# Expert visits of three token groups: a pair in half rows and a third group in quarter rows

## What is computed

```python
top_val, top_idx = lax.top_k(t @ w_router + b_router, 4)        # 4 of 32 experts for each token
g = jnp.minimum(xb @ w_gate[e] + b_gate[e], 7.0)
u = jnp.clip(xb @ w_up[e] + b_up[e], -7.0, 7.0)
act = g * jax.nn.sigmoid(1.702 * g) * (u + 1.0)
y = act @ w_down[e] + b_down[e]                                 # each of the three is 1024 x 1024
out = out.at[row_tok].add(y * row_w[:, None])
```

## Time and profile before

| | us |
|---|---|
| median of 3 runs | 1359.2 |
| lowest, highest | 1358.0, 1360.04 |
| the profiled execution, its own time | 1355.8 |
| its span (first to last instruction) | 1354.0 |
| TensorE matmul busy | 1295.7 |
| VectorE busy | 485.8 |
| ScalarE busy | 212.3 |
| GpSimd busy | 175.7 |

### The profile page before, as it was taken

The page is one execution under the profiler, slowest core; times in us unless marked ns, Lnnn a source line. Parts: engine busy times, 40 slices in busy tenths (PEclk is TensorE's granted clock), DMA queues, the critical chain, the costliest instruction groups (busy, mean ns, idle before and its releaser), DMA issues.

```text
span 1354.0 us, 25510 instructions
## 1 busy us (share of the span) xinstructions
PE 1295.7 (96%) x10704; PEld 630.4 (47%) x10704; DVE 485.8 (36%) x1124; ACT 212.3 (16%) x458; POOL 175.7 (13%) x138
## 2 busy tenths in 40 slices
PE   8999989998999999999999999999999998999995
PEld 3455565565554555555454543333333333344342
DVE  1875586755322222322322222322331322242221
ACT  2132244331101001110111110110110001001010
POOL 0031320001202120110110220010010010011002
PEclk9999999997899999999999999999999999999998
DMA  9300520236999999999999999999999999999996
GB/s 375 125 1 0 189 79 1 79 139 248 336 353 394 408 404 407 411 404 413 408 409 414 410 409 411 416 405 418 417 406 418 418 403 418 414 413 399 413 412 245
DMA packets 77924, 448.26 MB, mean 331 GB/s; under 512 B 13080, under 2 KB 16392, under 8 KB 28656
## 3 DMA queue, kind: packets, MB, share of 16 engines
q1 hardware_dynamic: 63936, 426.51, 76.8%
q0 software_dynamic: 13296, 17.98, 5.6%
q10 hardware_dynamic: 576, 2.10, 0.4%
HBM read 442.61 MB, written 14.94 MB: 338 GB/s over the span
## 4 chain that ended last, share of the span: by engine, by line
PE 59%; SPq 26%; DVE 6%; DMA 5%; issue 2%; ACT 1%; POOL 1%; POOLq 0%; ACTq 0%; DVEq 0%
PE pair L2027 38%; SPq L701 26%; PE pair L1857 4%; PE pair L1759 4%; PE pair L1720 3%; DMA ring<-in_w_gate 2%; DMA ring<-in_w_down 2%; DVE rest L1168 2%; PE pair L1981 2%; DVE rest L1199 1%; PE pair L1953 1%; PE pair L1994 1%; PE pair L1715 1%; DVE rest L1417 1%; POOL ring L812 1%
## 5 line engine op out<-in xcount | busy, mean ns | idle before, releaser
L2027 PE MATMUL pair<-ring,rest 128*32 128x256 f32 (+1 forms) x7952 | 833.8, 444 | 19.9 <-DMA ring<-in_w_down 12.9
L2027 PEld LDWEIGHTS pair<-ring,rest 128*32 128x32 f32 (+1 forms) x7952 | 332.6, 118 | 437.1 <-issue 288.9
L1168 DVE TENSOR_TENSOR rest<-pair,rest 128x512 f32<-128x512 f32 (+3 forms) x133 | 100.0, 755 | 421.7 <-PE pair L2027 386.6
L870 POOL DMA_INDIRECT out<-rest x57 | 89.7, 1573 | 742.9 <-ACT rest L1125 637.7
L1125 ACT ACTIVATE rest<-rest 128x256 f32<-128x256 f32 (+1 forms) x57 | 31.8, 596 | 512.2 <-DVE rest L1168 512.2
L1107 ACT ACTIVATE rest<-rest 128x512 f32<-128x512 f32 (+3 forms) x34 | 24.4, 718 | 304.6 <-DVE rest L1532 304.6
L1486 DVE TENSOR_SCALAR rest<-pair,rest 96x1 int32<-96x1 f32 (+2 forms) x34 | 7.3, 214 | 178.4 <-PE pair L1953 167.0
L1759 PE MATMUL pair<-ring 128*128 128x512 f32 (+1 forms) x192 | 69.4, 521 | 0.0
L1168 DVE TENSOR_TENSOR rest<-rest 128x512 f32<-128x512 f32 (+8 forms) x85 | 57.1, 683 | 32.1 <-ACT rest L1107 26.7
L2027 PE MATMUL pair<-rest 128*32 128x256 f32 (+1 forms) x592 | 62.1, 439 | 1.8 <-DMA rest<-in_w_down 1.8
L1720 PE MATMUL pair<-ring 128*128 128x512 f32 x128 | 58.1, 613 | 5.8 <-DMA ring<-in_w_in 5.8
(11 more groups left out here) (192 smaller groups left out, 841.3 us busy)
## 6 DMA issues: line engine op xcount, KB each, us to landing
ring<-in_w_gate SPq DMA_DIRECT2D x121, 1024.0 KB, 23.8
ring<-in_w_down SPq DMA_DIRECT2D x121, 1024.0 KB, 27.4
ring<-in_w_up SPq DMA_DIRECT2D x119, 1024.0 KB, 27.7
rest<-in_w_up SPq DMA_DIRECT2D x9, 1024.0 KB
rest<-in_w_gate SPq DMA_DIRECT2D x7, 1024.0 KB
rest<-in_w_down SPq DMA_DIRECT2D x7, 1024.0 KB
ring<-in_w_in SPq DMA_DIRECT2D x8, 520.0 KB, 8.5
ring<-in_x SPq DMA_DIRECT2D x8, 512.0 KB, 13.0
```

The lines of the kernel that those rows point to most:

```text
L870: p.indirect_dma_start(out=out_halves if w == HW else out_rows, out_offset=bass.IndirectOffsetOnAxis(ap=sidx[vi.ring][:, n:n + 1].bitcast( ...
L1168: return v.tensor_tensor(out=out, in0=a, in1=b, op=op)
L2027: last = T.matmul(ps[q * tn:(q + 1) * tn, col:col + w], x, pieces[slot][:, kk, q * w:(q + 1) * w], start=(k == 0 and col % 512 == 0), stop ...
```

## The change

Visits with three groups now have one pair and one single instead of three singles. Where a visit has a single beside its pair, each half of the pair is done by two stationaries of 32 tokens with the same 512 columns, instead of one of 64 tokens. Then a k-step has four matmuls of 32 tokens and 512 columns (partitions from 0, 32, 64 and 96) and four of 32 tokens and 256 columns. Visits with one, two, four groups and the overflow loop are as before. By way of `pairs` the same visits get two result parts instead of three: in `index`, `replicate`, `places`, `plus_bias`, `weigh`, `scatter` and `biases`.

```diff
-        scattered = [sum(g if (g := VISITS[w][1]) % 2 else g // 2 for w in range(v)) for v in range(NV + 1)]
+        scattered = [sum((VISITS[w][1] + 1) // 2 for w in range(v)) for v in range(NV + 1)]
 
         def pairs(vi):
-            return 0 if vi.j is None or vi.G % 2 else vi.G // 2
+            return 0 if vi.j is None else vi.G // 2
...
-                    blocks = {(0, 4): gm_c[:, 2:6], (2, 0): gm_c[:, 0:2], (0, 3): gm_c[:, 2:5],
+                    blocks = {(0, 4): gm_c[:, 2:6], (2, 0): gm_c[:, 0:2], (1, 1): gm_c[:, 0:5:4],
                               (0, 1): gm_c[:, 2:3]}[pairs(vi), singles(vi)]
...
+                            step = TOK if singles(vi) else tn
                             for q in range(DM // w):
-                                last = T.matmul(ps[q * tn:(q + 1) * tn, col:col + w], x,
-                                                pieces[slot][:, kk, q * w:(q + 1) * w],
-                                                start=(k == 0 and col % 512 == 0), stop=(k == KT - 1),
-                                                skip_group_check=True)
+                                for t in range(0, tn, step):
+                                    last = T.matmul(ps[q * tn + t:q * tn + t + step, col:col + w], x[:, t:t + step],
+                                                    pieces[slot][:, kk, q * w:(q + 1) * w],
+                                                    start=(k == 0 and col % 512 == 0), stop=(k == KT - 1),
+                                                    skip_group_check=True)
```

## The result

The changed kernel takes 1361.3 us (median of 20 runs, 1355.0 to 1366.4) against 1358.5 us (20 runs of the kernel before, 1353.9 to 1364.2): ratio 1.0022, 95% interval 1.0011 to 1.0032. By the ratio that is **3.0 us slower**, where 1.3 us faster was forecast (the medians themselves are 2.7 us apart). Its profiled execution took 1357.9 us (span 1356.0).

The account below looks back on a forecast made before the run. TensorE's releases were taken to pace transfers until about 420 us, the 16 DMA engines to bound afterwards. Terms -0.2 + 1.2 + 0.15 - 2.0 - 0.4 = -1.3 us gave 1357.9 us from 1359.2, range 1354.5 to 1362.0.

Parts of the forecast that it names:

- replicate: At three-group visits, a second short TensorE matmul costs what the first does; three visits before 420 us count: +1.2 us.
- What bounds the kernel: Expert phase: TensorE's releases pace transfers until about 420 us, then DMA engines bound and TensorE has up to 21 us reserve.
- Scattered rows: Scatters of three-group visits: 2304 small rows become 1152 large ones, cheaper for the DMA engines: -2.0 us.
- instruction code: Instruction queue: 3456 fewer load and matmul records mean less code to fetch; middle estimate -0.4 us.
- Product instructions: Three-group products: 512-column rounds save 3 ns each; only the five products before 420 us count: -0.2 us.
- VectorE: Longer bias additions and shuffles, hidden by products except in the wait between positions 0 and 1: +0.15 us.
- C: Rival: changing between 512 and 256 columns within a k-step costs a bubble; +22 us, 1381; chance 0.08.
- D: Rival: the four stationaries in three-group products don't run four at a time; 185 us over 27 products; chance 0.02.
- A: Rival: TensorE really leads until 757 us, so all nine replicates count; +1.4 us, 1360.6; chance 0.12.
- B: Rival: scatters cost the weight stream more than their own engine time; -3.3 us, 1355.9, faster; chance 0.2.

Follow-up runs that it names:

- split_all: Changed kernel with the pair's 512-column matmuls cut into 256-column ones in all 27 three-group products: 1362.4 us, ratio 1.0034 to the kernel before.
- before_rep2: Kernel before with replicate of three-group visits cut into two matmuls: 1363.4 us, ratio 1.0039 to the kernel before.
- before_warm: Kernel before with three matmuls that nothing reads in TensorE's waits ahead of the first product: 1359.5 us, ratio 1.0001.
- before_hooks_later: Kernel before with the three pieces of small work of gate(0) put one k-step later: 1358.5 us, ratio 1.0004.
- split_first: Changed kernel with the pair's 512-column matmuls cut to 256 columns in position 0's gate product alone: 1360.5 us, ratio 1.0017 to the kernel before.
- after_warm: Changed kernel with three matmuls that nothing reads in TensorE's waits ahead of the first product: 1362.5 us, ratio 1.0031 to the kernel before.
- after_rep1: Changed kernel with replicate of every three-group visit as one matmul again: 1354.7 us, ratio 0.9972 to the kernel before.
- v0_one: Changed kernel with one replicate matmul at position 0 only, two at the other eight three-group visits: 1355.8 us, ratio 0.9984 to the kernel before.
- hooks_later: Changed kernel, both replicate matmuls kept, with the small work of gate(0) put one k-step later: 1355.4 us, ratio 0.9992 to the kernel before.
- v0_two: Changed kernel with two replicate matmuls at position 0 only, one at the eight later three-group visits: 1358.7 us, ratio 1.0003 to the kernel before.

## Why the prediction was wrong, point by point

**The term that failed is replicate, "+1.2 us".** I priced the second matmul by its own duration, at position 0 "in a stretch whose granted clock averages 0.79", and took that clock as given. The profile had the warning: gate(0) ran into a change of the clock, at 2.79 us for the first k-step and 1.50 for the third. The second matmul itself cost a little less than priced (a pause of 0.94 us against 0.53, so 0.41 and not 0.53). But the clock then came back 10.2 us later, and 10.2 us at half speed are 5.1 us of work. The start part measures it: 70.1 us against a mean of 64.1 in the four profiles of before, **+6.0 us where the sum had +1.15** (-0.2 + 1.2 + 0.15). With one matmul it is 64.8, +0.7. The transfers were held up as much: the point with 359.5 MB of weights still to come lies 88.4 and 88.1 us behind the first product in the changed kernel, 82.1 to 82.5 in the four of before.

**What bounds the kernel: right.** TensorE's start counted in full, and later TensorE work hardly at all. In the changed kernel TensorE was about 5 us late through position 13 (position 13's gate starts at 746.9 us, 742.2 before), and the end only 2.0 us; in between it stopped waiting for weights (820 to 880 us above). That is the reserve. How fast the weights come behind the start doesn't depend on TensorE: see the 170 MB below. The sync queue's waits from 343 to 430 us went from 72.1 to 75.5 us.

**Scattered rows, "-2.0 us", and instruction code, "-0.4 us": right in kind; the first was forecast over twice too large, the second at less than half.** From 400 to 820 us:

```profile
DMA packets 27577, 171.23 MB, mean 408 GB/s; under 512 B 4224, under 2 KB 5356, under 8 KB 7641
...
q0 software_dynamic: 5156, 7.65, 7.8%
```

5356 - 4224 = 1132 rows of 1 KB are left, where I said 540. I had filled every pair with 64 tokens. But BLOCK_AT (L173) gives the pair the first and third block of an expert's tokens and the single the second, which is full. So 1708 small rows became 854 large ones; at the rows' prices, 1708 x 103 - 854 x 178 ns = 24 engine-us, 1.5 us.

**Both terms against the transfers.** A cleaner measure than the rest part, in which a late TensorE makes some time good, is how long the same weights take in the saturated time. Here are the queues while 170 MB of weights move (from 359.5 to 189.5 MB before the last), in the kernel before (425.69 to 860.91 us), the changed one (429.92 to 863.29) and split_all (431.58 to 865.87):

```profile
q1 hardware_dynamic: 23345, 170.01, 94.0%
q0 software_dynamic: 6406, 7.65, 7.7%
q8 instruction: 42, 0.69, 0.6%
...
q1 hardware_dynamic: 23345, 170.01, 94.2%
q0 software_dynamic: 5189, 7.59, 7.4%
q8 instruction: 30, 0.49, 0.4%
...
q1 hardware_dynamic: 23346, 170.02, 94.1%
q0 software_dynamic: 5190, 7.59, 7.4%
q8 instruction: 42, 0.69, 0.6%
```

They take 435.2 us in the kernel before, 433.4 in the changed kernel and 434.3 in split_all. The same stretch took 435.2 to 435.3 us in all eight profiles with the scatters of before (before_rep2, before_warm and before_hooks_later among them), and 433.3 to 433.4 in all nine with the changed scatters and 512-column products. split_all has the changed scatters with as many matmuls as before, so it parts the two terms, in one profile:

- *Scattered rows:* 435.2 - 434.3 = **0.9 us, where the sum had 2.0**. The stretch holds the scatters of all but the first of the nine visits. Half a microsecond of the miss is the count of rows above. The rest is that the transfers gained less than the rows' own time: the software queue's time in the stretch fell from 33.5 to 31.9 us (summed over packets, by 16), 1.6 us. Why only 0.9 of it came through stays open.
- *Instruction code and what goes with 3456 fewer records:* 434.3 - 433.4 = **0.9 us, where the sum had 0.4**. The middle of 0.7 and nothing was too low. The instruction queue's bytes fell from 1.43 to 1.21 MB, 15% for 13.4% fewer instructions. Its own time in the stretch fell from 2.7 to 1.9 us, nearly the whole 0.9. This is also why split_all is slower than split_first.

Together 1.9 us against the 2.4 of the sum. The rule of the Trainium skill that 512 B are enough for line rate (DMA: Bandwidth & Descriptors, Specifications) would have given nothing for the rows. The 0.9 us of split_all speak against it for accumulating rows, though no run changed the rows alone.

**Product instructions, VectorE:** a k-step of 1.29 us as forecast; the wait for L1548 reads 1.4 us as before, so its 0.15 us isn't visible in a tenth. Nothing else waited for VectorE, although its busy time rose by 19 us.

**The rivals.** C (a bubble at each change of columns, slower) had the right side and the wrong mechanism: the k-step refutes it. D is refuted by the same row. A is refuted by before_rep2: its nine extra matmuls made TensorE 1.4 us later between position 2's and position 13's gate products, and the 170 MB took 435.2 us as before. B's -3.3 us isn't there. No rival of mine had the clock in it, so the 0.16 for slower was too little for a change that puts work into a stretch at the edge of the clock.

The parts as measured, +6.0 - 1.9, give +4.1; the ratio gives +3.0. That 1361.3 us lies inside the range is luck: the range allowed the start 0 to 1.4 us, and it cost 6.0. The direction was wrong, and the 1 us between the parts and the ratio isn't explained.

## What to carry to other kernels

Price small work on TensorE not only by its duration but by where it stands: here a short matmul between the first long ones under the low clock cost over ten times the 0.4 us that it added, by delaying the return of the full clock. Look in the timeline for the instruction at which durations halve, and leave the stretch ahead of it unbroken; put replicates, dispatches and the like behind it or into one matmul. And where transfers lead most of the time, a few microseconds at the start, before anything stands in line, weigh more than many later.

## What the runs showed that I had not expected

A second short matmul between products kept TensorE at 1.2 GHz for 10.2 us longer, in all five profiles of the changed kernel and its variants with two replicate matmuls in both early pauses (the changed kernel twice, split_first, split_all, after_warm), and in none of the ten profiles that had one matmul in the first pause (before four times, before_warm, before_hooks_later, after_rep1 twice, v0_one) or no pause there (hooks_later). v0_two and the second profile of before_rep2 have 27.3 us; the first profile of before_rep2, where the clock came back ahead of the pause, has 17.1. When the product began doesn't sort them: 15.0 to 15.9 us after the fall of the clock in the five, 14.9 to 16.5 in the ten. Three short fillers in the waits ahead of the first product did not shorten it.

What stays open: after_rep1 is 0.28% faster than before (3.8 us), while start and rest, averaged, explain only +0.7 - 1.4 = -0.7 us of it. In its two profiles the first product starts at 341.1 and 342.0 us against 342.5 to 343.5 before, because the wait for the first gathered rows is shorter: 6.1 and 6.9 us from the gather's issue to the first transpose, against 7.2 to 7.6. That wait varies from 6.1 to 7.8 us over the 18 profiles and is as short in the changed kernel's first (6.3) and in before_rep2's first (6.1), so that it isn't a trait of after_rep1; the difference stays unexplained.
